# Decode step of a hybrid attention and MoE layer: adaLN tiles inside the projection's weight stream, key pages over three slots, prompt units three to a tile

## The reference, cut to what matters

```
mod  = silu(c) @ w_ada + b_ada                     # adaLN: 1024 x 6144, six vectors (shift1, scale1, gate1, shift2, scale2, gate2)
h    = LN(x) * (1 + scale1) + shift1
qa, ka, va, qb, kb, vb, ga, gb = split(h @ w_in)   # 1024 x 5888
oa   = block-sparse attention, 8 heads:            # samples over 2048 cached keys (paged), top 3 of 8 blocks by q.mean(k)
ob   = dilated windows (1, 4, 16), 4 heads each    # samples over 128 strided rows of three state buffers
mix  = (sigmoid(ga)*(oa @ w_proj_a) + sigmoid(gb)*(ob @ w_proj_b)) @ w_out
x    = LN1(alpha*x + gate1*mix)
x    = LN2(alpha*x + gate2*moe(LN(x)*(1+scale2)+shift2))   # 32 experts, top 2, 512 wide
```

## Time and profile before

| | kernel before |
|---|---|
| median of three executions | 1153.28 us |
| profiled execution | 1150.1 us, span 1148.0 |
| TensorE matmul busy | 857.3 us (75%) |
| VectorE busy | 344.4 us (30%) |
| ScalarE busy | 182.8 us (16%) |
| moved by DMA | 396.30 MB, mean 345 GB/s |
| chain that ended last | PE 43%, DMA 40%, DVE 10%, issue 3% |

### The profile page before, as it was taken

How to read it: one execution, slowest core, us unless ns; L and a number is a source line. 1 busy time by engine, 2 the same in 40 slices (tenths; PEclk the granted TensorE clock), 3 DMA queues, 4 the chain that set the end, 5 groups by cost and what they waited for, 6 DMA issues and landing times.

```text
span 1148.0 us, 11653 instructions
## 1 busy us (share of the span) xinstructions
PE 857.3 (75%) x4564; PEld 471.4 (41%) x4564; DVE 344.4 (30%) x520; ACT 182.8 (16%) x429; POOL 118.5 (10%) x116
## 2 busy tenths in 40 slices
PE   7699688999865999992600787777777777787740
PEld 5584466478752444882500332222222222232210
DVE  2057899827511331318310100000000000000008
ACT  2312123221221210001400211011101111111110
POOL 1212111202000222000020000000000000000020
PEclk9799899999976886897655999999999999999985
DMA  9987777566697999999998599999999999999931
GB/s 316 397 284 293 273 289 262 223 232 218 231 395 317 429 418 350 342 355 379 373 358 311 204 425 425 426 427 426 424 425 426 424 426 425 425 426 425 425 125 56
DMA packets 64740, 396.30 MB, mean 345 GB/s; under 512 B 6194, under 2 KB 8774, under 8 KB 41479
## 3 DMA queue, kind: packets, MB, share of 16 engines
q1 hardware_dynamic: 50544, 307.46, 67.8%
q0 software_dynamic: 12016, 85.90, 19.2%
q10 hardware_dynamic: 2144, 2.44, 0.6%
HBM read 387.89 MB, written 58.10 MB: 388 GB/s over the span
## 4 chain that ended last, share of the span: by engine, by line
PE 43%; DMA 40%; DVE 10%; issue 3%; ACT 1%; SPq 1%; ACTq 1%; POOL 0%; POOLq 0%; DVEq 0%
DMA ring<-in_w_exp_up_dram 26%; PE bank L764 11%; PE bank L405 8%; PE bank L415 3%; DMA ring<-in_cache_k_pages_dram,pidx 3%; DMA ring<-in_w_ada_dram 3%; PE bank L596 3%; DMA listed_tokens<-v,didx 3%; PE bank L679 3%; DVE ring L1141 2%; DMA ring<-in_w_in_dram 2%; DVE S L1145 2%; DMA v<-listed_tokens 2%; PE bank L666 1%; PE bank L457 1%
## 5 line engine op out<-in xcount | busy, mean ns | idle before, releaser
L764 PE MATMUL bank<-ring,hT 128*64 128x512 f32 x1024 | 241.9, 627 | 43.5 <-DMA ring<-in_w_exp_up_dram 41.0
L764 PEld LDWEIGHTS bank<-ring,hT 128*64 128x64 f32 x1024 | 88.8, 143 | 195.2 <-issue 195.2
L1525 DVE TENSOR_TENSOR hT<-hT,bank 128x256 f32<-128x256 f32 x32 | 19.3, 602 | 413.6 <-ACT hT L1068 413.6
L405 PE MATMUL bank<-hT,ring 128*128 128x264 f32 x576 | 139.2, 401 | 3.6 <-DMA ring<-in_w_in_dram 3.6
L782 PE MATMUL bank<-ring,hT 128*64 128x512 f32 x512 | 118.6, 604 | 19.5 <-DVE hT L1528 19.5
L405 PEld LDWEIGHTS bank<-hT,ring 128*128 128x128 f32 x576 | 112.1, 198 | 25.2 <-issue 6.0
L1141 DVE TENSOR_TENSOR ring<-ring,qbc 128x4096 f32<-128x4096 f32 x16 | 70.7, 4418 | 50.5 <-ACTq L809 41.6
L1663 POOL DMA_INDIRECT expert_rows<-work,ridx x32 | 31.1, 972 | 495.0 <-ACT work L801 371.0
L801 ACT ACTIVATE work<-bank 128x512 f32<-128x512 f32 (+5 forms) x83 | 36.6, 451 | 246.9 <-PE bank L782 145.2
L782 PEld LDWEIGHTS bank<-ring,hT 128*64 128x64 f32 x512 | 40.9, 138 | 76.6 <-issue 76.6
L1145 DVE TENSOR_REDUCE S<-ring 128x64 f32<-128x4096 f32 x16 | 70.6, 4413 | 0.2
(11 more groups left out here) (298 smaller groups left out, 781.2 us busy)
## 6 DMA issues: line engine op xcount, KB each, us to landing
ring<-in_w_exp_up_dram SPq DMA_DIRECT2D x32, 2048.0 KB, 22.0
ring<-in_w_exp_down_dram SPq DMA_DIRECT2D x32, 2048.0 KB, 21.8
ring<-in_w_exp_gate_dram SPq DMA_DIRECT2D x32, 2048.0 KB, 17.5
out_dram<-in_state_dil_kv_dram SPq DMA_DIRECT2D x8, 4064.0 KB
ring<-in_w_ada_dram SPq DMA_DIRECT2D x12, 2048.0 KB, 13.7
ring<-in_w_in_dram SPq DMA_DIRECT2D x11, 2048.0 KB, 17.1
out_dram<-in_state_dil_kv_dram SPq DMA_DIRECT2D x8, 992.0 KB
ring<-in_state_dil_kv_dram POOLq DMA_DIRECT2D x6, 1024.0 KB, 14.8
```

Of the source, the lines that this page charges most:

```text
L405: i = mm(bk[:, 0:NT], w[:, k, j * P:(j + 1) * P], hT3[:, k, :], start=(k == 0), stop=(k == KC - 1))
L764: i = mm(side(2, half).rearrange("p (m n) -> p m n", m=2), xT[s][:, k, :], w[:, :, k, half * 256:(half + 1) * 256], start=(k == 0), stop=( ...
```

## The change

Six of the late adaLN tiles (4 to 9) go between projection tiles, before tiles 3, 5, 8, 9, 10 and 11, in one stream of loads over slots 0 to 2; tiles 10 and 11 stay behind the projection. Each such tile's 64 matmuls (`ada_rows`, into bank 0 or 1) stand ahead of the projection tile, its transpose (`ada_turn`, bank 2 or 3) after that tile's first chunk. The prompt units stand three to a tile in tiles 2 to 6, and the five last steps are in tile 7. Key pages rotate over slots 4, 5 and 3; at turn 14 slot 3 takes the dilated keys of groups 0 and 1, for which page 11 must be reduced. Group 2's dilated keys are loaded when window step w1 is done. The dilated spreads, the block sums, penalties and maxima move to earlier chunks, and VectorE's order at the end becomes w0, halves 27 to 31, w1 to w5. The value page in slot 2 waits for the last projection tile.

```diff
--- before.py
+++ after.py
@@ -214,6 +214,7 @@
         w_full = [sem(f"w_full{i}") for i in range(6)]
+        k_full = [sem(f"k_full{i}") for i in range(3)]
         ew_full = [sem(f"ew_full{i}") for i in range(6)]
@@ -237,10 +238,15 @@
-        weights = [("ada", t) for t in range(4)] + [("win", t) for t in range(12)] \
-            + [("ada", t) for t in range(4, 12)] + [("wpa", 0), ("wpb", 0), ("wo", 0), ("wo", 1)]
-        WSLOT = {("ada", t): t if t < 4 else (t + 8) % 3 for t in range(12)}
-        WSLOT.update({("win", t): t % 3 for t in range(12)})
+        ADA_AT = {3: 4, 5: 5, 8: 6, 9: 7, 10: 8, 11: 9}
+        stream = []
+        for t in range(12):
+            stream += [("ada", ADA_AT[t])] if t in ADA_AT else []
+            stream += [("win", t)]
+        stream += [("ada", 10), ("ada", 11)]
+        weights = [("ada", t) for t in range(4)] + stream + [("wpa", 0), ("wpb", 0), ("wo", 0), ("wo", 1)]
+        WSLOT = {("ada", t): t for t in range(4)}
+        WSLOT.update({name: i % 3 for i, name in enumerate(stream)})
         WSLOT.update({("wpa", 0): 0, ("wpb", 0): 1, ("wo", 0): 2, ("wo", 1): 3})
@@ -248,9 +254,12 @@
         VSLOT = (4, 5, 2, 3)
-        for b in range(NB):
-            ring_take(("k", b, 0), 4)
-            ring_take(("k", b, 1), 5)
+        KSLOT = (4, 5, 3)
+        W_FIRST = 14
+        def key_turn(at):
+            return at if at < W_FIRST else at + 1
         ring_take(("vd", 0), 4, 2)
@@ -277,7 +286,8 @@
         Q_AFTER = {0: (0, 1), 1: (2,), 2: (3,), 3: (4,), 4: (5,), 5: (6,), 6: (7,)}
-        QBD_AFTER = {23: 0, 31: 1, 33: 2, 35: 3, 37: 4, 40: 5}
+        QBD_AFTER = {23: 0, 30: 2, 31: 3, 32: 4, 34: 5}
+        QBD_V = {(7, 2): 1}
         qbd = qbc[:, 2 * AW:4 * AW]
@@ -289,7 +299,8 @@
             return A_PARTS if u[0] == "a" else B_PARTS
-        STEPS = {2: (0, 1, 2), 3: (3, 4, 5, 6), 4: (7, 8, 9, 10), 5: (11, 12, 13, 14), 6: (15, 16, 17), 7: (18, 19)}
+        STEPS = {2: (0, 1, 2), 3: (3, 4, 5), 4: (6, 7, 8), 5: (9, 10, 11), 6: (12, 13, 14), 7: (15, 16, 17, 18, 19)}
@@ -379,6 +390,23 @@
+            def ada_rows(t, b):
+                w = landed(pe, ("ada", t)).rearrange("p (k n) -> p k n", k=KC)
+                bk = take(("adr", t), b)
+                for k in range(KC):
+                    for j in range(4):
+                        i = mm(bk[32 * j:32 * j + 32, 0:P], cT[:, k * 9:k * 9 + 32], w[:, k, j * P:(j + 1) * P],
+                               start=(k == 0), stop=(k == KC - 1))
+                done(("adr", t), i)
+                last_use[("ada", t)] = ("adr", t)
+            def ada_turn(t):
+                pe.wait_ge(s_modr, t + 1)
+                bk = take(("ada", t), 2 + t % 2)
+                done(("ada", t), tr(bk[:, 0:P], modr[t % 2], ident))
             pe.wait_ge(s_cT, 2)
@@ -527,6 +555,9 @@
                 width = 512 if t < 11 else 256
+                if t in ADA_AT:
+                    ada_rows(ADA_AT[t], acc[0] % 2)
+                    acc[0] += 1
                 w = landed(pe, name)[:, 0:KC * width].rearrange("p (k n) -> p k n", k=KC)
@@ -534,17 +565,21 @@
                             prompt_a(steps.pop(0))
+                        if (t, tt) in QBD_V:
+                            spread_b(QBD_V[t, tt])
                 for j in range(V_TILES[t][1] // P if t in V_TILES else 0, width // P):
...
                         spread_b(QBD_AFTER[4 * t + j])
+                    if j == 0 and t in ADA_AT:
+                        ada_turn(ADA_AT[t])
+                    if 4 * t + j == 40:
+                        block_sums()
                     if 4 * t + j == 42:
-                        block_sums()
-                    if 4 * t + j == 43:
                         penalties()
-                    if 4 * t + j == 45:
+                    if 4 * t + j == 44:
                         maxima()
@@ -563,22 +598,22 @@
-            ada(range(4, 5))
             pe.wait_ge(s_negm, 1)
...
             done("negm", mm(bk[0:NB, 96:96 + HS], e96, st96[0:96, 96:96 + HS], start=True, stop=True))
-            ada(range(5, 7))
+            ada_rows(10, 0)
+            ada_rows(11, 1)
+            ada_turn(10)
             pe.wait_ge(s_sum, 1)
...
             done("sum", mm(bk[0:96, 0:1], ownD[:, :], ones[0:NB, 0:1], start=False, stop=True))
-            ada(range(7, 8))
+            ada_turn(11)
             pe.wait_ge(s_rec, 1)
...
             done("rs", mm(bk[:, NB:2 * NB], work[0:96, 2432:2560], st96[0:96, 0:NB], start=True, stop=True))
-            ada(range(8, 12))
@@ -848,6 +883,19 @@
+            def ada_rows(t):
+                bk = filled(act, ("adr", t))
+                freed(("adr", t), copy(modr[t % 2], bk[:, 0:P]), s_modr)
+            def ada_turn(t):
+                bk = filled(act, ("ada", t))
+                for j in range(4):
+                    c = 4 * t + j
+                    i = A(mod[:, c, :], bk[:, 32 * j:32 * j + 9], ACT.Identity, bias=bT[:, c:c + 1])
+                freed(("ada", t), i, s_mod)
             ada(range(4))
@@ -923,9 +971,20 @@
+            def spread_b(jd):
+                for i_ in range(2):
+                    bk = filled(act, ("qbd", jd, i_))
+                    if jd and i_ == 0:
+                        act.wait_ge(s_kdmul, jd)
+                    i = A(qbd[:, i_ * 512:(i_ + 1) * 512], bk[:, :], ACT.Copy, scale=QSCALE)
+                    freed(("qbd", jd, i_), i, s_qbd)
             for t in range(12):
...
                 j0 = 0
+                if t in ADA_AT:
+                    ada_rows(ADA_AT[t])
                 steps = list(STEPS.get(t, ()))
@@ -948,14 +1009,10 @@
                     if c in QBD_AFTER:
-                        jd = QBD_AFTER[c]
-                        for i_ in range(2):
-                            bk = filled(act, ("qbd", jd, i_))
-                            if jd and i_ == 0:
-                                act.wait_ge(s_kdmul, jd)
-                            i = A(qbd[:, i_ * 512:(i_ + 1) * 512], bk[:, :], ACT.Copy, scale=QSCALE)
-                            freed(("qbd", jd, i_), i, s_qbd)
-                    if c == 42:
+                        spread_b(QBD_AFTER[c])
+                    if j == 0 and t in ADA_AT:
+                        ada_turn(ADA_AT[t])
+                    if c == 40:
                         bk = filled(act, "own")
@@ -981,14 +1038,14 @@
                 act.dma_start(st_out[g][0, :, P * DIL[g] - 1, 1].rearrange("s h d -> s (h d)"), v[0:NB, 2, c:c + 256]).then_inc(s_vout, 16)
-            ada(range(4, 5))
             act.wait_ge(s_sub, 1)
...
             A(own[:, 40:60], own[:, 40:60], ACT.Exp).then_inc(s_exp, 1)
-            ada(range(5, 7))
-            ada(range(7, 8))
-            ada(range(8, 12))
+            ada_rows(10)
+            ada_rows(11)
+            ada_turn(10)
+            ada_turn(11)
@@ -1133,11 +1190,13 @@
                 b, hh = at // 2, at % 2
-                kt = ring[:, 4 + hh, :]
+                kturn = key_turn(at)
+                kt = ring[:, KSLOT[kturn % 3], :]
                 if half == 0:
...
                         dve.wait_ge(s_qbc, b + 1)
-                    k3 = landed(dve, ("k", b, hh)).rearrange("p (k n) -> p k n", k=HPG)
+                    dve.wait_ge(k_full[kturn % 3], 16 * (kturn // 3 + 1))
+                    k3 = kt.rearrange("p (k n) -> p k n", k=HPG)
                     V.tensor_tensor(k3, k3, qbc[:, b % 2 * AW:(b % 2 + 1) * AW].unsqueeze(1).to_broadcast([P, HPG, AW]),
@@ -1201,12 +1260,11 @@
                     at += 1
-            for j in range(4):
+            window_scores(0)
+            for j in range(5):
+                page_scores(at + j)
+            for j in range(1, 6):
                 window_scores(j)
-                page_scores(at + j)
-            page_scores(at + 4)
-            window_scores(4)
-            window_scores(5)
@@ -1578,7 +1636,7 @@
             for hh in range(2):
-                page_half(k_pages, 0, hh, 4 + hh, w_full[4 + hh])
+                page_half(k_pages, 0, hh, KSLOT[hh], k_full[hh])
@@ -1591,25 +1649,27 @@
             filled(pool, last_use[("ada", 3)])
-            load_window(3, 0, 0, 0, s_kdw)
-            load_window(3, 1, 0, 2048, s_kdw)
-            for b in range(1, NB):
-                for hh in range(2):
-                    pool.wait_ge(s_kred, 2 * b + hh - 1)
-                    page_half(k_pages, b, hh, 4 + hh, w_full[4 + hh])
+            for at in range(2, 2 * NB):
+                n = key_turn(at)
+                if at == W_FIRST:
+                    pool.wait_ge(s_kred, W_FIRST - 2)
+                    load_window(KSLOT[W_FIRST % 3], 0, 0, 0, s_kdw)
+                    load_window(KSLOT[W_FIRST % 3], 1, 0, 2048, s_kdw)
+                if at >= 3:
+                    pool.wait_ge(s_kred, n - 2)
+                page_half(k_pages, at // 2, at % 2, KSLOT[n % 3], k_full[n % 3])
             pool.wait_ge(s_z, 20)
...
```

(4 more changed lines are left out.)

## The result

Six runs of the changed kernel beside six of the kernel before, on one chip: **1142.44 us** against 1151.04 us in the median, a ratio of 0.9924 with a 95% interval of 0.9898 to 0.9950. The prediction was 1142, in a range of 1126 to 1151.

What follows compares the result with a forecast made beforehand. Adjacent stages each leave idle what the other lacks; the sample start is projection end plus tail. The tail's 40.6 us less a projection ending 29.0 later gives 11.6 us: 1138.5 profiled, 1142 on the median, range 1126 to 1151.

Steps and rivals of the forecast that it cites:

- Tile 6 and the idle VectorE: In the projection: tile 6 starts at 183.8, 15.9 us earlier; VectorE then idles from 177.7 to 192.3 before unit 12.
- The wait at query spread 7: Before the last key transposes in the projection: TensorE, ready at 210.8, goes on only from 216.2, a stall of 5.4 us.
- The last pages: VectorE's last key pages: a 2.9 us wait for page 14, none for page 15; halves 28 to 31 end at 265.9.
- The new wait: Projection tile 7, dilated spread 3: TensorE stalls 21.8 us, from about 246 to 267.8, until VectorE's window step 1 has multiplied.
- The projection's end: Last projection chunk: 267.8 + 68.7 puts the projection's end at 336.5, 29.0 us later than before.
- The tail: Last projection chunk to sample start: 14.1 us instead of 54.7, giving 40.6 us; adaLN tiles 10 and 11 arrive free.
- rival C: No change: the tail keeps a load, tile 11 landing 16 us after the projection; gain 5, 1148 us; chance 0.18.
- The size: Whole kernel: sample start at 350.6 against 362.2, 11.6 us gained; 1142 us on the median of 1153.28.
- The third key slot: Key pages in the projection: the third slot removes waits like the 5.91 us one but by itself gains nothing.
- A: Projection: VectorE never waits on scores, TensorE does not stop at spread 3; gain 45, 1108; chance with half-stall case 0.13.
- B: Slower: page 15's late landing lengthens TensorE's stall; gain gone from 23.3 us after asking, 1160 us at 30; chance 0.07.

Runs made afterwards that it cites:

- four units: The changed kernel with prompt units four to a tile in tiles 3 to 5, as in the kernel before: 1119.7 us, ratio 0.9704.
- two key slots: The changed kernel with key pages over slots 4 and 5 alone, dilated keys of groups 0 and 1 in slot 3 from the start: 1152.7 us, 0.9999.
- Late spreads: The changed kernel with dilated spreads 2 to 5 after chunks 35, 36, 37, 39 instead of 30, 31, 32, 34: 1122.3 us, ratio 0.9725.
- halves earlier: The changed kernel with VectorE doing four page halves instead of one behind unit 11, and two behind window step 0: 1122.3 us, ratio 0.9738.
- pages held: The kernel of units and spreads with sample 0's two value pages issued behind the last chunks of projection tiles 8 and 9: 1115.0 us, ratio 0.9677.
- units and spreads: The changed kernel with prompt units four to a tile and dilated spreads 2 to 5 behind chunks 35, 36, 37, 39: 1124.0 us, ratio 0.9729.

## Why the prediction was right, step by step

**Tile 6 and the idle VectorE.** Predicted start of tile 6 183.8, measured 182.16. TensorE's waits for VectorE's weights in tiles 3 to 5 went, as said, but the text gave the credit to three units to a tile alone: of the 14.4 us in the kernel before, the third key slot without them leaves 3.3 (four units to a tile), and they without the slot leave 5.4 (two key slots). VectorE's idle time before unit 12 was put at 14.6 us (177.7 to 192.3) and is 16.63 (to 192.19). The wait at query spread 7 was put at 5.4 and is 5.16; the key transposes were said to wait 3.0 and waited 3.75.

**The last pages.** Window step 0 was put at 238.5, where half 26 ends (measured 238.37). Page 14's issue fell into a multiply as in the earlier trace rows, 4.93 us where the row had 4.40: the issue began at 234.46, inside the multiply (234.04 to 238.46), and was done 0.9 us behind its end. Its wait was put at 2.9 and is 1.65; page 15's was put at none, within 2.4, and is 1.59. The sum of the two, 3.24, is near the 2.9, so the second dilated multiply comes at 266.08; the text let it end at 267.1, that is begin at 265.9.

**The new wait.** Predicted 21.8 us, to 267.8, before the fourth dilated spread; measured 21.51, to 268.05. Late spreads, four units and halves earlier each remove most of it and gain 21.5 to 24.1 us more than the change. It was on the path, about one for one.

**The projection's end.** Predicted 336.5, measured 336.7. This is the term that the result hung on: 29.0 of the 40.6 us that the tail gives were said to go here, and 29.2 went.

**The tail.** Predicted 14.1, measured 17.2. The mis-sized term is the load of adaLN tile 11: the text had it "some 3 us after" the last chunk, "beside the chain and free", and TensorE waited for it until 345.74, 9.0 us after, with the sums' matmuls (L610, from 349.58) behind it in the list although VectorE had had them ready since 347.1. The outputs, exps and sums were sized rightly: 0.2, 5.0, 2.7 and 2.9 make 10.8 us, and the sums are ready 10.4 after the chunk. Tile 11 then costs 2.5 us (347.1 to 349.58), and the small steps from there to the first sample values take 4.3 where 3.3 was estimated. In late spreads, four units and pages held, where the stall is gone, tile 11 costs less: waits of 2.4 to 3.0 us and tails of 13.9 to 14.4, against 17.0 measured alike (from the last chunk's end). An earlier end of the projection is not what does it: with two key slots the projection ends 8.0 us later, the wait is 5.52 and the tail 14.3. Part of rival C thus came true, for 3 us.

**The size.** The start was predicted 11.6 us earlier and is 8.4 earlier; the median was predicted 11.3 below 1153.28 and is 8.6 below the 1151.04 of its own comparison. That the figure 1142 met the median of 1142.44 within 0.5 us is luck: the kernel before had 1153.28 over the three executions that the prediction started from and 1151.04 over all six, and this 2.2 us makes up for most of the gain that was missing. The mechanism and its places are right; the gain is over-sized by about 3 us, the tail's.

**The third key slot.** Here the text was wrong. It said that the slot "by itself gains nothing, because now the scores set VectorE's pace". With two slots the gain is gone (0.9999 against 0.9924, intervals apart). The failed step is the pace: without the slot the pages set it around 119 us, not the scores. The waits of 7.20 and 1.54 us are back. The first of them stands in VectorE's list ahead of weights of a unit, TensorE waits 5.36 us for these at 124.31, and by the end of the stall everything is 8.0 us late. That the slot waits fed the same chain as the stall was in the prediction's own list too (half 19 before query spread 6); it was not asked what the list looks like without the slot.

**The rivals.** A's condition, that VectorE never waits on scores, did not hold, and no run tests its price as it stands: the nearest, pages held, starts the sample values 37.1 us earlier, where A had 34 us and the 11.6 of the forecast, 45. The Trainium skill, Perfetto Trace Analysis, Optimization Strategy, says that a kernel whose busiest engine changes over time may gain by interleaving the regimes. It says that time may be gained, not how much. These runs agree with it once the orders are put right (0.9677), and show how little of it arrives before that (0.9924). B did not occur: page 15 landed 11.3 us after its issue, far from the 23.3 at which the gain would be gone.

## What to carry to other kernels

Work moved beside other work is paid at the next point where the engine's fixed list meets a wait: find that wait first, follow it through the engines to the one that is late, and count as cheap only what stands ahead of it. Price each part of a composite change by undoing it alone; here one part gave 27 us at the start of the next stage and the rest together lost 19, although one piece of that rest, the third key slot, was itself worth over 8. When a stall goes, look at what it had been keeping apart: transfers that used to be asked for during it now fall on the load that is needed next.

## What the runs showed of the hardware that I had not expected

A load that is asked for first is not there first. In units and spreads projection tile 9 (2 MB) was asked for at 240.87, behind adaLN tile 7 (2 MB, 238.95) on the same queue and 3 to 5 us ahead of a quarter window (1 MB) and two value pages (2 MB each) on GpSimd's. AdaLN tile 7 landed after 8.0 us, at 247.0, the quarter window at 254.0, the pages at 259.7 and 265.9, and tile 9 last, 25.6 us after its issue. These 9 MB at the 376 GB/s of the earlier trace rows take 25 us, so the tile came about when all of them had; with the pages issued later it landed after 14.5 us and nothing waited for it. The prediction had priced tiles 10 and 11 by their own bytes alone, 4.2 MB in 11 us. Two value pages are asked for behind them (337.64 and 338.94 in the timeline of the kernel after), and tile 11 let TensorE go on at 345.74 where that price gave some 3 us after 336.5. But the pages do not explain all of it: in late spreads they follow tile 11's issue at the same distance, 8.7 us, and it landed 13.5 us after its issue, where it took 16.8 in the change. Where these 3.3 us come from stays open.
